# Bias rows in DRAM: 32 copies in place of 16, stored later, and read in four wide transfers per half

## What is computed

```python
mod = c_act @ w_ada[l] + b_ada[l]
sh1, sc1, g1, sh2, sc2, g2 = [m[:, None, :] for m in jnp.split(mod, 6, axis=-1)]
h = rmsnorm(x, norm_gains[l, 0]) * (1.0 + sc1) + sh1
y = token_mixer(h, w_in[l], w_out[l], sinks[l], bias_hb)
...
s_own = jnp.einsum('bhqd,bhjd->bhqj', qc, k_own).astype(jnp.float32) * scale
dist = qpos[:, None] - (ob * MOBA_BLOCK + offs)[None, :]
s_own = s_own + bias_hb[:, t5_bucket(dist)][None]
s_own = jnp.where(dist >= 0, s_own, -jnp.inf)
```

## Time and profile before

| | |
|---|---|
| Median of three executions | 781.82 us (779.53 to 782.61) |
| Profiled execution, own time | 779.63 us |
| its span | 777.9 us |
| TensorE busy (matmul) | 740.6 us, 95% |
| VectorE, ScalarE busy | 514.2 us (66%), 445.0 us (57%) |
| HBM | 149.61 MB read, 1.44 MB written |
| Granted TensorE clock | full in all 40 slices |
| First phase, up to the MLP of block one | about the first 165 us |

### The profile page before, as it was taken

The page is one execution under the profiler, slowest core; times in us unless marked ns, Lnnn a source line. Parts: engine busy times, 40 slices in busy tenths (PEclk is TensorE's granted clock), DMA queues, the critical chain, the costliest instruction groups (busy, mean ns, idle before and its releaser), DMA issues.

```text
span 777.9 us, 12196 instructions
## 1 busy us (share of the span) xinstructions
PE 740.6 (95%) x4148; PEld 624.0 (80%) x4148; DVE 514.2 (66%) x746; ACT 445.0 (57%) x700; POOL 40.0 (5%) x70
## 2 busy tenths in 40 slices
PE   0699999999999999999999999999999999999998
PEld 0598966799999886777889777777788888888886
DVE  6887697788877743356657465665667777777443
ACT  0654678676666433355445687554546777776331
POOL 3000100100000100013110000000000000000000
PEclk9999999999999999999999999999999999999999
DMA  8999986257787655545764664544444666665651
GB/s 311 371 333 339 278 275 178 82 163 214 226 243 275 225 194 163 166 131 145 209 189 122 204 190 132 166 116 142 148 136 143 200 174 189 185 193 188 212 190 56
DMA packets 137423, 151.56 MB, mean 195 GB/s; under 512 B 6179, under 2 KB 111782, under 8 KB 137384
## 3 DMA queue, kind: packets, MB, share of 16 engines
q1 hardware_dynamic: 135566, 146.33, 60.1%
q10 hardware_dynamic: 1820, 4.74, 1.8%
HBM read 149.61 MB, written 1.44 MB: 194 GB/s over the span
## 4 chain that ended last, share of the span: by engine, by line
PE 48%; DVE 3%; issue 1%; ACT 1%; DVEq 0%; ACTq 0%
PE acc L1402 11%; PE acc L1410 9%; PE acc L1412 8%; PE acc L1411 8%; PE acc L1403 5%; PE acc L1390 1%; PE acc L1391 1%; PE acc L1389 1%; PE aux L1378 1%; DVE wl L975 1%; DVE rows_tmp L1266 1%; ACT wh L607 1%; DVE sig L1282 0%; DVE x_rows L1058 0%; PE aux L1581 0%
## 5 line engine op out<-in xcount | busy, mean ns | idle before, releaser
L975 DVE TENSOR_TENSOR wl<-raw,wh 128x1024 fp32r<-128x1024 f32 x217 | 266.2, 1232 | 151.6 <-ACT wh L607 150.7
L607 ACT ACTIVATE wh<-raw 128x1024 fp32r<-128x1024 f32 x217 | 228.0, 1055 | 124.9 <-PE acc L1412 112.8
L1389 PE MATMUL acc<-xT,wh 128*128 128x256 f32 x440 | 125.4, 285 | 3.3 <-DVE xT L1031 2.2
L1402 PE MATMUL acc<-xT,wh 128*128 128x512 f32 x352 | 124.5, 399 | 0.3 <-DVE xT L1013 0.3
L1390 PE MATMUL acc<-xT,wh 128*128 128x256 f32 x440 | 124.5, 283 | 0.0
L1391 PE MATMUL acc<-xT,wl 128*128 128x256 f32 x440 | 124.5, 283 | 0.0
L1410 PE MATMUL acc<-wh,xT 128*128 128x512 f32 (+1 forms) x272 | 108.6, 399 | 0.6 <-issue 0.3
L1412 PE MATMUL acc<-wh,xT 128*128 128x512 f32 (+1 forms) x272 | 104.4, 384 | 0.0
L1411 PE MATMUL acc<-wl,xT 128*128 128x512 f32 (+1 forms) x272 | 104.3, 384 | 0.0
L1403 PE MATMUL acc<-xT,wl 128*128 128x256 f32 x352 | 98.9, 281 | 0.0
L1389 PEld LDWEIGHTS acc<-xT,wh 128*128 128x128 f32 x440 | 84.4, 192 | 6.0 <-issue 2.6
(11 more groups left out here) (270 smaller groups left out, 894.6 us busy)
## 6 DMA issues: line engine op xcount, KB each, us to landing
raw<-in_w_in SPq DMA_DIRECT2D x66, 512.0 KB, 3.7
raw<-in_w SPq DMA_DIRECT2D x64, 512.0 KB, 4.3
raw<-in_w_ffn_in SPq DMA_DIRECT2D x44, 512.0 KB, 4.2
raw<-in_w_ada SPq DMA_DIRECT2D x27, 512.0 KB, 5.8
raw<-in_w_ffn_out SPq DMA_DIRECT2D x22, 512.0 KB, 4.3
raw_more<-in_w_ada SPq DMA_DIRECT2D x13, 512.0 KB, 6.5
raw<-in_w_out SPq DMA_DIRECT2D x13, 512.0 KB, 4.6
rows_tmp<-in_w_ada ACTq DMA_DIRECT2D x8, 512.0 KB
```

Source lines behind the costliest of these rows:

```text
L607: A(wh[:, s, :], raw_unit, ACT.Copy).then_inc(rounded, 1)
L975: V.tensor_tensor(wl[:, s, :], raw_slot(r), wh[:, s, :].bitcast(f32), ALU.subtract).then_inc(split_ready, 1)
L1389: mm(bank[:, 0:ROWS], wh[:, s, w], hi, start=(kt == 0), stop=False)
L1402: mm(bank[:, :], wh[:, s, w], moving[:, kt, :], start=(kt == 0), stop=False, skip_group_check=True)
```

## The change

`COPIES` goes from 16 to 32. The store so writes 786 KB in place of 393 KB, one read fills 32 partitions (256 KB), and a half takes four reads. The first half is read behind the load of unit 9 in place of unit 5. The store is issued by ScalarE behind the eight normalised columns of the input (`from_transposed_both`, which rounds units 1 and 2 on its way), in place of directly behind the copy of the rows; ahead of the rounding of unit 3. The second half stays behind unit 17.

```diff
-COPIES = 16
+COPIES = 32
...
-BIAS_AFTER = [5, 17]
+BIAS_AFTER = [9, 17]
...
             A(dist_rows[:, :], aux[1][0:N_HEADS, 0:DIST], ACT.Copy).then_inc(dist_copied, 1)
 
-            act.wait_ge(dist_copied, 1)
-            act.dma_start(bias_dram, dist_rows[:, :].unsqueeze(1).to_broadcast([N_HEADS, COPIES, DIST])).then_inc(dist_stored, 16)
             for r in range(RT):
...
             from_transposed_both(X_PROJ1, A1, modT[:, M_SH1:M_SH1 + KT], {5: 1, 7: 2})
+            act.wait_ge(dist_copied, 1)
+            act.dma_start(bias_dram, dist_rows[:, :].unsqueeze(1).to_broadcast([N_HEADS, COPIES, DIST])).then_inc(dist_stored, 16)
```

## The result

The change makes the kernel slower: 786.4 us as the median of eight executions (783.92 to 787.83) against 781.0 for eight of before, a ratio of 1.0065 (1.0048 to 1.0083). The forecast was 782.5, its range ended at 785.8. The profiled execution took 787.2 us with a span of 785.5, before 779.63 and 777.9: 7.6 us more on both counts. The median grew by 5.4: the profile shows one execution of each kernel, and single executions of one kernel lie up to 4 us apart here (783.92 to 787.83 after, 779.53 to 782.61 before), so the traces tell where time goes and the medians how much.

What follows compares the result with a forecast made beforehand. TensorE was taken to bind, with ScalarE and VectorE's ladder of sixteen heads setting its few waits. Terms 0 + 0 + 0.7 + 0 gave +0.7 us on the median of 781.82: 782.5 us, range 779.5 to 785.8.

Steps and rivals of the forecast that it cites:

- What bounds the kernel now: Whole kernel: TensorE, busy 95%, binds; ladder delays before 100 us reach the end; hurrying gains at most 2.3 us.
- Store issued later: ScalarE near 41 us: the 0.67 us issue fits into 0.85 us idle before the eviction at 42.03; 0 us.
- Twice the copies: Store from 40.9 to about 53.1 us: SyncE waits 1.6 us behind unit 9, no bandwidth lost; 0 us.
- Rival C: Behind unit 9: SyncE waits for a store landing at 60 us, TensorE stalls 5.9 us; 787.7 us, chance 0.13.
- First read moved: Behind unit 9: 5.0 us of engine time enters a full stretch; unit 10 lands at 62.5 us, covered for TensorE.
- credit of 1.6 us: Loads ahead of unit 9: a shorter queue without the first read lets weights land in 3.7 us against 5.3.
- cover of 2.9 us: Unit 10: ready at 64.8 us after landing, rounding and split, while TensorE wants it at 67.7.
- What is late next: Unit 16 lands 2.3 us late at 78.2, ScalarE 0.7 us late, passed to TensorE's wait at 103.67; +0.7 us.
- catch-up of 1.1 us: Between units 10 and 16: engines at 399 GB/s against 371 make good 7% of 16 us.
- Second read: Behind unit 17, eight issues to four: unit 18 still waits for ada 26; 0 us (0 to -0.7).
- B: Both reads: wider reads are cheap, a half takes 2.6 us, unit 16 on time; 781.5 us, chance 0.32.
- D: Second read: its crowding makes unit 18 late, all 2.3 us of TensorE's waits might go; 779.5 us, chance 0.07.

Runs made afterwards that it cites:

- after_store_early: The changed kernel with the store back at its early place in ScalarE's program; 785.49 us, 1.0071 of the kernel before.
- copies_only: The kernel before with only COPIES raised from 16 to 32, store and first read at their old places; 782.81 against 780.09 us, 1.0037.
- read_behind_9_only: The kernel before with only the first read moved from behind unit 5 to behind unit 9; 782.93 us, 1.0040.
- after_again: The changed kernel run once more, unedited, on another occasion; 784.64 us, 1.0077 of the kernel before.
- after_spin: The changed kernel with eight unread matmuls added in TensorE's gap near 30 us; 1.0078 of the kernel before.
- wide_store_16: The kernel before with its 16 copies stored from all 128 partitions instead of 16; 783.05 against 780.17 us, 1.0041.
- wide_16_second_19: The kernel before with 16 copies stored from 128 partitions and the second half read behind unit 19 in place of 17; 1.0049.

## Why the prediction was wrong

The sum was +0.7 us, and 5.4 were measured. Two of its terms were far too small: twice the copies, put at 0, cost 2.7 us, and the moved first read, put at 0.7 us with what follows from it, cost 2.8 us.

**What bounds the kernel now.** Right: everything was made before 172 us, and the stages behind kept their lengths. Wrong in one sentence: "Whatever delays a rung before 100 us delays the end". A rung's delay passes on only where TensorE has less of its own: 6.4 us on ScalarE cost 2.3 us beyond the 4.4 that TensorE was already late.

**Store issued later, 0.** Right within the intervals, by `after_store_early` against the changed kernel (5.4 and 5.4 us).

**Twice the copies, 0.** This step failed, by 2.7 us. Its duration was nearly right (12.2 us foreseen, 9.9 measured), and so was the doubling of the data: 8.8 us foreseen, and 528 packets at 127 per 2 us come to 8.3. What failed is what those 8 us cost the others. I took the engine time of the store of before, 1.3 us for 272 packets, 75 ns each, and charged the doubled store as much again. In `copies_only` the 182 packets between 26 and 28 us took 49.6% of the engines, 87 ns each; the 251 of the next 4 us took 0.732 x 4 x 16 / 251 us = 187 ns each, and in the changed kernel all of them did (0.90 x 6 x 16 / 381 = 227 ns). And I wrote that no bandwidth is lost "up to about 54.6 us", thinking of SyncE's wait alone. The wait did not happen, the loss did: at 99 GB/s instead of 361 for 6 us, an estimated 4 us of loading, or 3 if the time before 42 us, when little was waiting, is left out. The earlier trace rows held a warning: 124 packets, 0.19 MB, in 2 us is 95 GB/s, in a stretch that moved 399. I read the share of 27.8% beside it and not the rate. That a packet would come to cost the engines two or three times as much no row of before showed. Rival C had the sign, and with 787.7 us nearly the time, but by luck: SyncE never waited for the store, the stall of 5.9 us never came, and half of the loss was the read's.

Here the rule weighed on the reads belonged. By the Trainium skill (SBUF — State Buffer, Door 1: The DMA port swizzle) sixteen neighbouring partitions move some 109 GB/s; the store from 16 partitions ran at 98 to 100 in three kernels and from 128 at 0.65 MB in 2 us, so the runs agree for the store in its steady state (0.28 MB in its first 2 us in `copies_only` is 140). For the reads, by the order tried, they do not.

**First read moved.** Its 5.0 us of engines was right in size: 1.05 MB at 216 GB/s. Unit 10 landed at 67.7, not 62.5; in `read_behind_9_only`, without the larger store, it was rounded at 65.17, in place of 59.59: 5.6 us later, where 3.4 had been allowed. The credit of 1.6 us was not paid. The cover of 2.9 us for TensorE failed with it: with rounding and split unit 10 was ready at about 70.0 us, 2.3 us behind the 67.7 at which TensorE was to want it. TensorE waited 0.38 us for it in the profiled execution, already made late by its clock, 1.72 in `after_again` and 2.35 in `after_spin`: the gap before 73 us that the prediction had named as a sign of being wrong.

**What is late next.** The catch-up of 1.1 us did not come either. Each following unit makes ScalarE wait (1.74 us at unit 16): SyncE issues a weight when a slot comes free, and a slot comes free only when a late unit was used. What unit 10 is late, unit 16 is late: 5.87 us of waiting, 6.4 us at unit 16, where 0.7 was forecast; with the read alone 3.9 (81.40). Then the "3.1 without credit and catching up" of this step (5.0 - 1.6 is 3.4) was the nearest term to the truth, and I kept it for the range only. Nor did the place hold: I passed the delay to the wait at 103.67 (head 4), and it came out at head 3, which had no wait and hence no row.

**Second read, 0.** Right for the kernel before, where the second read costs TensorE nothing. Not looked at: once the ladder is late, unit 18 behind the second read is what TensorE waits for, and 2.2 us of the loss can be had back there.

**B** was wrong: reads of 32 rows move 216 to 235 GB/s over the 4 to 6 us shown, little more than the 209 of 16 rows; 300 had been its mark. **D** was wrong: halving unit 18's wait gains nothing that holds.

**A term that no part of the sum had** is the clock behind a grown wait. By the lags it makes at most 0.9 us of the profiled execution's 7.6, and none in `read_behind_9_only`; the slope over all executions would allow 1.9 of 5.4. Its share stays open. That `copies_only` lost 5.5 us in its profiled execution and 2.7 in the median is in part scatter that the traces show: its store was issued 1.0 us late before anything had changed, the trace of before is an early one, and the wait for the last ada chunk is 3.98 and 3.97 us in two traces with the early doubled store but 1.19 in a third.

## What to carry to other kernels

Before a transfer is doubled, divide its bytes in one window by the window: a rate far under that of its neighbours may be a ceiling of its own, and the time behind it may be taken from every queue that shares the engines. A late load in a ring whose slots come free one by one is handed down whole, so give no credit for catching up unless a row shows spare engine time. Where two engines work down a chain of steps and wait for each other, keep a lag for each of them and look at every rung for the larger one, the rungs without a wait included.

## What the runs showed of the hardware

A store of 1.5 KB rows from 16 partitions ran at 98 to 100 GB/s while holding 90% of the sixteen engines' time; from 40 to 46 us no packet of SyncE's queue stood beside its 381, although loads had been issued at 40.45 and 42.72. The Trainium skill (DMA: Bandwidth & Descriptors, Queues, rings and completion order) has an engine take turns between queues by whole packets of at most 64 descriptors; the store's 528 packets in the profile are 33 for each of 16 engines, so the runs are consistent with one turn of that size, and not with its typical one of 9 to 17. The early store left 21% to the other queue, which one such turn would not explain.

Reads of 1 KB rows ran at 169 to 216 GB/s in five kernels whatever their order, start or width (16 or 32 rows); the highest of the stretches shown was 235, with wide reads.

TensorE's granted clock was at the 1.2 GHz level (0.50 to 0.51) from about 108 to 113 us in the changed kernel, behind a wait of 2.29 us. The wait's length alone does not decide: one of 1.38 us at 103.35 in `wide_store_16` was followed by 0.70 over 10 us, one of 1.44 us at 109.47 in `wide_16_second_19` by a full clock.
